# Gate and up rows in runs of 4 KB, and ten down pieces held outside the ring of raw weights

## What is computed

```python
for e in range(N_EXPERTS):                                   # 32
    hid = jax.nn.silu(jnp.matmul(h, w_gate[e])) * jnp.matmul(h, w_up[e])   # (1024, 256) each
    out = out + jnp.matmul(hid, w_down[e]) * combine[:, e:e + 1]           # (256, 1024)
```

## Time and profile before

| | |
|---|---|
| median of 3 runs | 2043.73 us |
| the profiled execution | 2044.95 us, span 2043.3 us, mean granted clock 0.994 |
| PE busy | 1957.5 us, 96% of the span |
| PEld / DVE / ACT / POOL busy | 83% / 57% / 51% / 15% |
| read from memory | 239.57 MB |
| experts, first gate/up to last down matmul | 514 to 814 us |

### The profile page before, as it was taken

One profiled execution on the slowest core, in us unless ns is written; L12 is line 12 of the kernel. 1 busy time (PEld: TensorE's weight loads), 2 busy tenths in 40 slices (PEclk: granted clock), 3 DMA queues, 4 the chain that ended last, 5 costly groups with the idle time before them and its releaser, 6 DMA issues.

```text
span 2043.3 us, 27995 instructions
## 1 busy us (share of the span) xinstructions
PE 1957.5 (96%) x10551; PEld 1687.6 (83%) x10551; DVE 1172.9 (57%) x2306; ACT 1037.0 (51%) x1705; POOL 312.9 (15%) x420
## 2 busy tenths in 40 slices
PE   7999999999999998999999999999999989999998
PEld 7977877777777776789999999999788777877887
DVE  3345388554999998744444444444444536736772
ACT  4654534444788787654444444444443555345341
POOL 2601232011000001201120112011010002402310
PEclk9999999999999999999999999999999999999999
DMA  4411221146899999412222222222244312122121
GB/s 147 143 44 40 73 78 58 42 149 230 295 368 362 359 372 350 144 47 75 73 70 70 67 74 70 70 69 93 75 159 134 124 42 65 39 62 67 59 103 42
DMA packets 178017, 255.58 MB, mean 125 GB/s; under 512 B 13565, under 2 KB 92234, under 8 KB 177882
## 3 DMA queue, kind: packets, MB, share of 16 engines
q1 hardware_dynamic: 168832, 221.33, 33.0%
q0 software_dynamic: 8784, 31.92, 4.2%
q10 hardware_dynamic: 266, 0.52, 0.1%
HBM read 239.57 MB, written 14.16 MB: 124 GB/s over the span
## 4 chain that ended last, share of the span: by engine, by line
PE 78%; DVE 11%; ACT 5%; DMA 3%; issue 2%; POOL 0%; SPq 0%; ACTq 0%; DVEq 0%
PE pb L2405 51%; PE pb L2433 6%; PE pb L2776 5%; DVE wlo L1574 3%; PE pb L2799 3%; PE pb L3000 2%; PE pb L2919 2%; ACT whi L951 2%; PE pb L2489 2%; PE pb L2502 2%; PE pb L2908 2%; DMA wraw<-w_down 1%; DMA wraw<-w_up 1%; DVE arena L2179 1%; PE pb L3019 1%
## 5 line engine op out<-in xcount | busy, mean ns | idle before, releaser
L2405 PE MATMUL pb<-whi,AT_hi 128*128 128x512 f32 (+4 forms) x1992 | 777.5, 390 | 13.5 <-DVE arena L2179 5.4
L1574 DVE TENSOR_TENSOR wlo<-wraw,whi 128x1024 fp32r<-128x1024 f32 (+4 forms) x430 | 490.3, 1150 | 518.0 <-ACT whi L951 513.6
L2405 PE MATMUL pb<-whi,AT_lo 128*128 128x512 f32 (+4 forms) x1992 | 726.7, 365 | 0.0
L2405 PE MATMUL pb<-wlo,AT_hi 128*128 128x512 f32 (+4 forms) x1992 | 725.1, 364 | 0.0
L951 ACT ACTIVATE whi<-wraw 128x1024 fp32r<-128x1024 f32 (+4 forms) x446 | 440.7, 993 | 381.6 <-PE pb L2405 319.7
L2405 PEld LDWEIGHTS pb<-whi,AT_hi 128*128 128x128 f32 x1992 | 376.7, 189 | 65.0 <-issue 17.3
L2405 PEld LDWEIGHTS pb<-wlo,AT_hi 128*128 128x128 f32 x1992 | 377.1, 189 | 44.3 <-issue 6.5
L2405 PEld LDWEIGHTS pb<-whi,AT_lo 128*128 128x128 f32 x1992 | 375.4, 188 | 45.0
L2433 PE MATMUL pb<-arena 128*128 128x128 f32 (+1 forms) x1180 | 177.4, 278 | 27.3 <-ACT arena L987 6.2
L2433 PEld LDWEIGHTS pb<-arena 128*128 128x128 f32 (+1 forms) x1180 | 143.9, 145 | 62.9 <-ACT arena L1051 9.1
L2776 PE MATMUL pb<-whi,AT_hi 128*128 128x512 f32 x256 | 103.6, 405 | 1.5 <-DVE AT_lo L1920 1.5
(11 more groups left out here) (315 smaller groups left out, 2375.1 us busy)
## 6 DMA issues: line engine op xcount, KB each, us to landing
wraw<-w_in_a SPq DMA_DIRECT2D x288, 128.0 KB
wraw<-w_gate SPq DMA_DIRECT2D x128, 256.0 KB
wraw<-w_up SPq DMA_DIRECT2D x128, 256.0 KB
wraw<-w_down SPq DMA_DIRECT2D x58, 512.0 KB
wraw<-w_in_b SPq DMA_DIRECT2D x40, 512.0 KB
wraw<-w_in SPq DMA_DIRECT2D x28, 512.0 KB
wraw<-w_mem_kv SPq DMA_DIRECT2D x16, 512.0 KB
wraw<-w_in_a SPq DMA_DIRECT2D x16, 512.0 KB
```

Source lines behind the costliest of these rows:

```text
L1574: dve.tensor_tensor(w_slot(wlo, p, p % SPL), raw_slot(p), w_slot(whi, p, p % SPL).bitcast(F32), ALU.subtract).then_inc(lo_done[p % SPL], 1)
L2405: mm = pe.matmul(ACC[bank][:, 0:n], a, b, start=kc == 0 and q == 0, stop=i == c["count"] - 1 and kk == per - 1 and q == 2)
```

## The change

- **Runs of 4 KB.** A partition of a gate/up piece now holds four neighbouring rows (1024 numbers, 4 KB) of one matrix: even pieces are gate, odd ones up. A piece is one DMA. ACT and DVE still make the old layout (gate half, up half) in `whi` and `wlo`: for piece p they read one half of each of the two raw slots of the pair (`raw_halves`). So ACT's copy waits for both pieces of the pair (`both_of`), and the load into either slot of a pair waits until both pieces of the pair that was there are split.
- **x_col and the gains** follow the new row order: each transpose takes every fourth number of a token's row (j = 4).
- **Ten held pieces** instead of six: both down pieces of experts 4, 10, 16, 22 and 28. Six lie in the columns used before, with loads at the places used before. Four lie in `h2T`; SP waits for `rt_mm` after the experts' piece 3 and loads them there, ahead of piece 4.

```diff
--- before.py
+++ after.py
@@ -238,15 +238,16 @@
         P_MOE = len(pieces)
 
         NEXP = NGRP * EPG
+        HELD_EXPERTS = (4, 10, 16, 22, 28)
         EXPERT_ORDER = [what for n in range(NEXP + 1)
                         for what in ([("gu", n, q) for q in range(4)] if n < NEXP else []) + ([("dn", n - 1, b) for b in range(2)] if n else [])]
         piece_of = {what: P_MOE + j for j, what in enumerate(EXPERT_ORDER)}
-        by_pair = lambda w: w.rearrange("e (q p j) f -> e q p (j f)", p=P, j=2)
-        gate_rows, up_rows = by_pair(A["w_gate"][0]), by_pair(A["w_up"][0])
+        by_four = lambda w: w.rearrange("e (q p j) f -> e q p (j f)", p=P, j=4)
+        gate_rows, up_rows = by_four(A["w_gate"][0]), by_four(A["w_up"][0])
         down_rows = A["w_down"][0].rearrange("e (b p) d -> e b p d", p=P)
         for kind, ex, q in EXPERT_ORDER:
             if kind == "gu":
-                pieces.append(([(512 * i, 512, w[ex, q].unsqueeze(1)) for i, w in enumerate((gate_rows, up_rows))], 1, PIECE))
+                pieces.append(([(0, PIECE, (gate_rows, up_rows)[q % 2][ex, q // 2].unsqueeze(1))], 1, PIECE))
             else:
                 pieces.append(([(0, D, down_rows[ex, q].unsqueeze(1))], 1, D))
 
@@ -298,8 +299,8 @@
         def slot_cols(p):
             return pieces[p][1] * pieces[p][2]
 
-        NHELD = 6
-        HELD = [P_MOE + 14 + 24 * i for i in range(NHELD)]
+        HELD = [piece_of["dn", n, b] for n in HELD_EXPERTS for b in range(2)]
+        NHELD = len(HELD)
         RING = [p for p in range(NP) if p not in HELD]
         HELD_AT = chunks[CH["out1"]]["first"]
         ring_at = lambda p: p - sum(h < p for h in HELD)
@@ -309,6 +310,25 @@
             if p in HELD:
                 return held[HELD.index(p)][:, 0:slot_cols(p)]
             return wraw[:, ring_at(p) % RAW, 0:slot_cols(p)]
+
+        GU = {piece_of["gu", n, q]: q % 2 for n in range(NEXP) for q in range(4)}
+        assert all(ring_at(p) % 2 == GU[p] and p not in HELD for p in GU)
+
+        def both_of(p):
+
+            return [p - GU[p], p - GU[p] + 1] if p in GU else [p]
+
+        def raw_halves(p):
+
+            if p not in GU:
+                return raw_slot(p)
+            a = ring_at(p - GU[p]) % RAW
+            return wraw[:, a:a + 2, 512 * GU[p]:512 * GU[p] + 512]
+
+        def split_slot(buf, p):
+
+            w = w_slot(buf, p, p % SPL)
+            return w.rearrange("p (w c) -> p w c", w=2) if p in GU else w
 
         def raw_loaded(p):
 
@@ -465,6 +485,7 @@
         c_moe = take(C_MOE - C_BASE)
         before, iota_g, iota_s, empty, tok1, mod4, by4 = (const(k, c_moe, C_BASE) for k in ("before", "iota_g", "iota_s", "empty", "tok1",
                                                                                             "mod4", "by4"))
+        h2T_at = top[0]
         h2T = take(4096, KD, T)
         gen_d = view(top[0], 2048, 2, D)
         gen_d_end = top[0] + 2048
@@ -514,7 +535,7 @@
         gen_sil = take(1024, 2, T)
         gen_hid = take(1024, 2, T)
         x_row = [big[:, D * i:D * i + D] for i in range(2)]
-        x_col = [x.rearrange("s (q c j) -> s q j c", c=P, j=2) for x in x_row]
+        x_col = [x.rearrange("s (q c j) -> s q j c", c=P, j=4) for x in x_row]
         row_pair = lambda a, r: a[:, r:r + 2, :].rearrange("p a b -> p (a b)").rearrange("p (k s) -> p k s", k=KD)
         xg_hi, xg_lo = ([row_pair(a, 2 * i) for i in range(2)] for a in (AT_hi, AT_lo))
         hd_hi, hd_lo = ([a[:, 4, FF * i:FF * i + FF] for i in range(2)] for a in (AT_hi, AT_lo))
@@ -532,7 +553,7 @@
         mem_at = a0 + 19712
         assert mem_at >= moe_top
         assert mem_at + 2304 + 2048 <= n_arena
-        held = [view(at + 1024 * i, 1024) for at, n in ((mem_at + 2304, 2), (gen_at, 2), (big_at + 2048, 2)) for i in range(n)]
+        held = [view(at + 1024 * i, 1024) for at, n in ((mem_at + 2304, 2), (gen_at, 2), (big_at + 2048, 2), (h2T_at, 4)) for i in range(n)]
         memx = [view(mem_at, 2048, 2, D), take(2048, 2, D)]
         junkD = view(top[0], 1024)
         km_tok = [view(mem_at, 1024, 2, 512), take(1024, 2, 512)]
@@ -704,8 +725,8 @@
             def load(p):
                 loads, per, n = pieces[p]
                 if p not in HELD and ring_at(p) >= RAW:
-                    before = RING[ring_at(p) - RAW]
-                    sp.wait_ge(lo_done[before % SPL], before // SPL + 1)
+                    for before in both_of(RING[ring_at(p) - RAW]):
+                        sp.wait_ge(lo_done[before % SPL], before // SPL + 1)
                 dst = raw_slot(p).rearrange("p (k n) -> p k n", k=per)
                 share = 96 // len(loads)
                 for c0, w, src in loads:
@@ -719,7 +740,11 @@
                     load(HELD[1])
                 if p == HELD_AT + 3:
                     sp.wait_ge(norm_ss, so_far("mem0", 1, 2))
-                    for h in HELD[2:]:
+                    for h in HELD[2:6]:
+                        load(h)
+                if p == P_MOE + 3:
+                    sp.wait_ge(S("rt_mm"), 1)
+                    for h in HELD[6:]:
                         load(h)
 
 
@@ -780,8 +805,8 @@
                 return pool.tensor_tensor(x2, v[2], v[3], ALU.add)
 
             with nc.allow_non_contiguous_dma(reason="gains as columns"):
-                pool.dma_start(g_moe.rearrange("p (q j) -> p q j", j=2),
-                               A["norm_ffn_g"][0].rearrange("(q p j) -> p q j", p=P, j=2)).then_inc(S("g_moe_in"), 16)
+                pool.dma_start(g_moe.rearrange("p (q j) -> p q j", j=4),
+                               A["norm_ffn_g"][0].rearrange("(q p j) -> p q j", p=P, j=4)).then_inc(S("g_moe_in"), 16)
             link(pool.memset(qaT[96:P], 0.0))
             link(pool.memset(kaT[96:P], 0.0))
             pool.wait_ge(S("consts"), 16)
@@ -945,10 +970,11 @@
 
                 if p >= NP:
                     return
-                act.wait_ge(*raw_loaded(p))
+                for b in both_of(p):
+                    act.wait_ge(*raw_loaded(b))
                 if p >= SPL:
                     act.wait_ge(piece_used, p - SPL + 1)
-                act.activation(w_slot(whi, p, p % SPL), raw_slot(p), ACT.Copy).then_inc(hi_done, 1)
+                act.activation(split_slot(whi, p), raw_halves(p), ACT.Copy).then_inc(hi_done, 1)
 
             def during(j, fed=0):
                 for i in range(fed, chunks[j]["count"] - 1):
@@ -1571,7 +1597,7 @@
                 if p >= NP or lo_by_pool(p):
                     return
                 dve.wait_ge(hi_done, p + 1)
-                dve.tensor_tensor(w_slot(wlo, p, p % SPL), raw_slot(p), w_slot(whi, p, p % SPL).bitcast(F32),
+                dve.tensor_tensor(split_slot(wlo, p), raw_halves(p), split_slot(whi, p).bitcast(F32),
                                   ALU.subtract).then_inc(lo_done[p % SPL], 1)
 
             def during(j, fed=0):
@@ -2756,7 +2782,7 @@
 
                 if i == 0:
                     pe.wait_ge(S(f"x_row_in{g % 2}"), 16 * (g // 2 + 1))
-                transposes("moe", 2 * g + i, [x_col[g % 2][:, 2 * i + k // 2, k % 2, :] for k in range(4)])
+                transposes("moe", 2 * g + i, [x_col[g % 2][:, i, k, :] for k in range(4)])
 
             def gate_up(n, qs):
                 g, e = n // EPG, n % EPG
```

## The result

The changed kernel took 2066.48 us (median of 4 runs, 2065.29 to 2069.79) against 2046.36 of the kernel before (4 runs, 2040.54 to 2049.68): a ratio of 1.0098, 95% interval 1.0074 to 1.0122. It is slower by 20 us, outside the predicted range; what happened is rival 1. The profiled execution took 2067.0 us, span 2065.3. Its page has PE busy 1961.0 us, 3.5 more than before, in a span longer by 22.0.

The account below looks back on a forecast made before the run. PE's pace through the experts was taken as the bound, with DMA stalls on top. Terms -6.1 + 2.5 + 3.0 = -0.6 us gave 2044.3 against the profiled 2044.95, or 2043 against the median; range 2031 to 2058.

Parts of the forecast that it names:

- rival 1: Experts' ring: pairs landing later than x = 5.5 us set the pace; 2056 at 6.0, 2110 at 7.8; chance 0.18.
- What bounds the kernel: Experts: PE sets the pace, 8.97 us an expert undisturbed; transfer stalls add 6.1 us over seven groups.
- Term 1: Experts' DMA: 4 KB runs and four more held pieces cheapen transfers, ending stalls: -6.1 us (0 to -6.1).
- Term 2: Experts' ring: both slots come free only after the second split, some rounds late: +2.5 us (0 to +20).
- Term 3: Transposes of every fourth number, on PE's path: slower weight loads, +3.0 us (0 to +8).
- Term 4: Ahead of the experts: four held loads end before the first gather; 0, or +2 if they run into it.

Follow-up runs that it names:

- deep rings: Four further ring slots for experts' pieces: changed kernel with six held pieces, five pairs, 2045.93 us; kernel before, ten single slots, 2043.66 us.
- the square above: Four kernels with ten held pieces, ratios to the kernel before: 2 KB single slots 1.0023, 4 KB single 0.9998, 2 KB pairs 1.0153, 4 KB pairs 1.0098.
- the later issue: Kernel before, with four held down pieces issued after the fourth gate/up piece, at about 476 instead of 456.5: 2043.87 us, ratio 0.9986.
- the two waits alone: Kernel before with ten held pieces, plus one wait for both pieces of a pair: SP's alone 2062.25 us, ACT's alone 2059.94 us.

## Why the prediction was wrong

**What bounds the kernel** held: PE's pace through the experts, DMA's stalls on top. Both deep rings show 35.92 us a group where I read 35.87 as undisturbed.

**Term 1, the cheaper transfers: wrong in size.** The price of 39.9 engine-us a MB for all 4 KB runs, from the POOL rows, doesn't hold. After the change, 530 to 800:

```profile
q1 hardware_dynamic: 22516, 81.98, 84.5%
q0 software_dynamic: 1728, 6.29, 5.9%
```

that is 0.845 x 16 x 270 / 81.98 = 44.5, against 44.6. Like with like, with the same number of slots and held pieces: 43.3 against 44.1 in the two deep rings (first the five pairs, then the ten single slots)

```profile
q1 hardware_dynamic: 24225, 88.22, 88.5%
q1 hardware_dynamic: 41105, 89.19, 91.1%
```

and 44.1 against 45.4 with single slots and ten held pieces, 2 to 3% less. I took half of the 15% from a row of another queue with other work. The Trainium skill (DMA: Bandwidth & Descriptors, Why small descriptors are slow), by whose fixed cost I had estimated a saving of near 2%, which I set aside, was right in size here. The DMA share did fall to 0.90, near the 0.92 I named, but for another reason, so the agreement is luck: the queue was idle since SP could not issue. A low share was no sign of room. And the held pieces, which I credited with 5.8 us of DMA time, cost 4.5 us of stage by themselves.

**Term 2, the pairs: the right mechanism, and the step that failed.** I charged 2.5 us for the pairs; by the square above they cost 20 us. I sized a round as 4.0 us away and 5.3 landing, 9.3 against the 9.47 that the ring could afford (287 / 30.3), a margin of 2%. Both terms were too small. The 4.0 left out the two additions of the sums (1.20 us) that DVE does between the splits of an expert's second pair, which was away for 4.8 us. (The first pair has only the product between its splits, and my 4.0 held for it: it had landed by 637.84 and its slots were loaded again at 641.76.) In the round shown the landing, 4.9 us, was even below my 5.3, and the round still passed 9.47. And 5.3 leaned on idle time of DMA that did not make the landings short: the sixteen loads of up weights in the chain of work from 520 to 815 took 4.3 to 7.1 us, 5.4 in the mean, and each pair's gate half is issued some 0.45 us ahead of its up half, so 5.9 for the pair. 4.8 + 5.9 is 10.7 (of the landings that were waited for). With the measured mean of 275.6 / 28 = 9.84 us an expert, my own formula gives 9.84 x 32 / 30.3 = 10.4 us for a round instead of 9.3. Rival 1 at x = 6 had the stage at 303 us; it was 9.84 x 32 = 315. Rival 1's test, groups over 36.7 us, was met: 577.33 to 619.76 is 42.4. The error was one of weighing: where a loop has 2% to spare and its landing is known only between 4.7 and 7.8, the range must hold the case in which it is the bound with far more than 0.18.

**Term 3, the transposes: nothing, where I had +3.0.** Groups take 35.92 us in both deep rings, the one with every second number and the one with every fourth. Weight loads of every fourth number in the changed kernel:

```profile
L2459 PEld LDWEIGHTS pb<-arena x48: 197/210/213, 583.0 to 786.8; 128*128 128x128 f32 x48
```

8 ns over the median of every second number, not 63. The 139 ns that I read there as the time of contiguous numbers is the shortest load of that same group; the sixteen loads of contiguous rows at 489.1 to 492.3 took 139 to 143 ns, 141 in the median, so the step is the same. Of the rule in the Trainium skill (Advanced Engine Details and Errata, Memory Cachelines) this case now shows the whole of a step: 141 ns for contiguous numbers, 202 for every second, 210 for every fourth. The penalty is there, but nearly all of it is paid at the first step, not where the page's rule of two hits in a line puts it.

**Term 4, ahead of the experts: right in the sum, not in its parts.** I had the four held loads done by 503. They were issued at 499.00, and DMA's share was 1.02 from 504 to 508, so they met the gather; yet it was no later for PE (5.5 us from issue to first transpose, 5.6 before), and from the gather to the first down matmul it is 24.1 us in both. The stage began 1.3 us later, which, as far as the traces tell, is the balance of two losses that I had not seen. The changed kernel lost time to a wait of 2.89 us for `w_mem_kv`, where the profile of before has 0.24. The kernel before lost time to a granted clock of 0.59 from 496 to 500: its gather waited 14.98 us, where it was 13.39 in the changed kernel. The kernel before with the later issue has neither and issues the gather at 503.84; against that the changed kernel was 2.4 us late and the one before 1.2.

## What to carry on

A wait for both of two buffers costs twice, as the two waits alone showed (9 to 10 us each): each load is issued later and each use begins later. Before pairing buffers of a ring, write one round down, every instruction between the landing and the release on each engine included, and compare it with the pace of the consumer; with a few per cent to spare count it as the bound. When all engines and DMA fall together, look for such a loop, and test it with more slots, not with faster transfers: four more slots were worth 26 us with pairs and some 3 without; runs of twice the length were worth about 5 us in the short ring of single slots and, with their pairs, nothing in the deep one. And what is loaded long ahead must not be issued in front of what is needed next: moving four such loads by 20 us was worth 3 to 5 us in each of two kernels.

## What the chip showed that I had not expected

- Runs of 4 KB in place of 2 KB took 2 to 3% less engine time a MB (43.3 against 44.1, 44.1 against 45.4), not 15%.
- Transposes' weight loads: 141, 202 and 210 ns for contiguous numbers, every second and every fourth.
- With five pairs in the ring DMA moved 379 GB/s from 630 to 670 while PE kept its pace. And ten single slots kept it at a DMA share of 0.98 to 1.00, so a share of 0.99 in the stage of before did not show that the rate was the limit.
- A gap of some 3 us in PE's work, 470 us into the kernel, was followed by 4 us at a granted clock of 0.51 and 4 at 0.64, and the gather came 5.3 us later than in the kernel without the stall of 3.8 us on ACT. A gap was not always what came first: in the profile of before the clock was 0.59 from 496 to 500, and PE had been busy in all of 484 to 496.
